# Stick-breaking input projection: the first four weight pieces move into the MLP stage before it

## The reference

```python
for i in range(DEPTH):                      # DEPTH = 2
    h = rmsnorm(x, norm_mix[i])
    ...                                     # mixer: i == 0 latent attention, i == 1 stick-breaking
    x = x + out
    h = rmsnorm(x, norm_mlp[i])
    x = x + jnp.square(jax.nn.relu(h @ mlp_w_up[i])) @ mlp_w_down[i]
y = rmsnorm(x, norm_final)

def sb_mixer(h, q_pos, past_k, past_v, w_in, w_o):
    qkv = (h @ w_in).reshape(B, S, 3, SB_HEADS, SB_HEAD_DIM)
    ...
```

## Time and profile before

| what | value |
|---|---|
| median of three runs (lowest to highest) | 2772.87 us (2772.1 to 2774.59) |
| the profiled execution's own time | 2770.23 us |
| its span, first to last instruction | 2768.4 us |
| TensorE busy | 2665.2 us, 96% of the span, 14531 matmuls |
| VectorE, ScalarE, GpSimd busy | 1733.3, 1155.4 and 732.1 us |
| mean granted TensorE clock | 0.988 of full speed |
| DMA engines busy | 41.5% of the span |

### The profile page before, as it was taken

The page is one execution under the profiler, slowest core; times in us unless marked ns, Lnnn a source line. Parts: engine busy times, 40 slices in busy tenths (PEclk is TensorE's granted clock), DMA queues, the critical chain, the costliest instruction groups (busy, mean ns, idle before and its releaser), DMA issues. The chain is left out here.

```text
span 2768.4 us, 40402 instructions
## 1 busy us (share of the span) xinstructions
PE 2665.2 (96%) x14531; PEld 2236.2 (81%) x14531; DVE 1733.3 (63%) x2331; ACT 1155.4 (42%) x2260; POOL 732.1 (26%) x627
## 2 busy tenths in 40 slices
PE   7989998999999989999899999998999999899998
PEld 6879887788888878888798877776878888788886
DVE  5656666376555688898310008887475555688887
ACT  4334445343333433344322219997343333333433
POOL 3200001135444400001221116665154445300001
PEclk9999999999999999999999999999999999999999
DMA  4311122514444573442235448764234444655342
GB/s 149 88 60 45 45 83 84 190 54 152 137 145 141 189 241 122 160 136 101 86 128 160 145 112 194 174 161 140 91 99 138 145 140 138 235 175 164 126 155 100
DMA packets 285877, 368.81 MB, mean 133 GB/s; under 512 B 25984, under 2 KB 205696, under 8 KB 285696
## 3 DMA queue, kind: packets, MB, share of 16 engines
q1 hardware_dynamic: 285696, 366.42, 41.5%
HBM read 242.19 MB, written 124.16 MB: 132 GB/s over the span
## 5 line engine op out<-in xcount | busy, mean ns | idle before, releaser
L2338 DVE TENSOR_TENSOR x<-m_ps,x 128x1024 f32<-128x1024 f32 x224 | 273.3, 1220 | 92.6 <-PE m_ps L79 92.5
L2047 POOL TENSOR_TENSOR m_u<-m_u,m_u 128x512 f32<-128x512 f32 x128 | 179.5, 1413 | 347.7 <-DVE m_u L2181 342.7
L1994 POOL TENSOR_SCALAR m_stat<-m_stat 128x1 f32<-128x1 f32 x36 | 12.0, 334 | 838.8 <-ACT m_sqjunk L1938 674.4
L2169 DVE TENSOR_TENSOR m_z<-m_ps,m_part 128x512 f32<-128x512 f32 x96 | 66.3, 691 | 143.5 <-PE m_ps L79 143.2
L1800 ACT COPY m_part<-m_ps 128x512 f32<-128x512 f32 x96 | 56.3, 587 | 204.8 <-PE m_ps L79 204.8
L2157 DVE TENSOR_TENSOR m_up<-m_upr,m_up 128x512 fp32r<-128x512 f32 x128 | 87.8, 707 | 28.5 <-ACT m_up L1787 28.5
L3296 ACT ACTIVATE e_b<-e_ps 128x512 f32<-128x512 f32 (+3 forms) x192 | 95.8, 499 | 12.3 <-PE e_ps L3514 11.7
L1787 ACT CAST m_up<-m_upr 128x512 fp32r<-128x512 f32 x128 | 75.6, 615 | 57.9 <-PE m_ps L79 57.9
L3298 ACT ACTIVATE e_ps<-e_ps 128x512 f32<-128x512 f32 (+3 forms) x192 | 96.3, 502 | 0.0
L2027 POOL TENSOR_TENSOR m_uprS<-m_upr 128x512 f32<-128x512 f32 x62 | 94.8, 1529 | 4.9 <-DVE m_upS3l L2157 4.9
L3579 PE MATMUL e_ps<-ident,e_b 128*128 128x128 f32 x576 | 94.7, 274 | 0.7 <-POOL e_b L3394 0.6
(11 more groups left out here) (1192 smaller groups left out, 9183.1 us busy)
## 6 DMA issues: line engine op xcount, KB each, us to landing
scratch_u<-m_u SPq DMA_DIRECT2D x224, 256.0 KB, 2.1
m_ur<-scratch_u SPq DMA_DIRECT2D x208, 256.0 KB, 2.7
m_upr<-in_mlp_w_up SPq DMA_DIRECT2D x32, 1024.0 KB, 5.8
m_wr<-in_mlp_w_down SPq DMA_DIRECT2D x64, 512.0 KB, 6.5
scratch_x<-x SPq DMA_DIRECT2D x18, 512.0 KB, 2.6
x<-scratch_x SPq DMA_DIRECT2D x8, 1024.0 KB, 9.0
scratch_qr<-a_qrst SPq DMA_DIRECT2D x9, 512.0 KB, 3.4
a_x<-in_x_prompt SPq DMA_DIRECT2D x8, 512.0 KB, 4.9
```

What stands on the lines that cost most here:

```text
L2047: pool.tensor_tensor(u_st[out][:], u_st[a][:], u_st[b][:], op).then_inc(u_summed.sem, 1)
L2338: dve.tensor_tensor(out, bank[:, at:at + 2, :], out, ALU.add).then_inc(summed.sem, 1)
```

## The change

Four things are done. SyncE loads pieces 2 and 3 of group 0 in the MLP stage too, behind a wait for product P6 of the last pass (their places in memory are those of operands that P6 is the last to read). ScalarE makes the high parts of pieces 0 and 1 between its last tiles of the MLP stage. GpSimd makes the low part of piece 0 at the end of its MLP program, behind a wait for VectorE's last `scale_2`. In the projection stage the counters of these parts are set by hand, ScalarE makes high parts 2 and 3, and VectorE the low parts of pieces 1, 2 and 3.

```diff
@@ output_and_mlp_stage
-        ahead = [place(f"ahead{j}", shape, raw0_at + 4 * KIB * j) for j in range(2)]
+        ahead = [place(f"ahead{j}", shape, raw0_at + 4 * KIB * j)[:] for j in range(2)]
+        if not final:
+            ahead += [raw[:] for raw, _, _ in next_w[2:]]
...
+        next_in = [] if final else [signal(f"next_in{j}") for j in range(2)]
+        next_hi_done = [] if final else signal("next_hi")
...
                 for j, piece in enumerate(ahead):
-                    sp.dma_start(piece[:], rows[:, 2 * j:2 * j + 2, 0:HALF_TOK]).then_inc(next_in.sem, 16)
+                    if j == 2:
+                        sp.wait_ge(down.sem, down_at(LAST_G, "P6"))
+                    sp.dma_start(piece, rows[:, 2 * j:2 * j + 2, 0:HALF_TOK]).then_inc(next_in[j // 2].sem, 16)
             sp.wait_ge(wt_lo["T1"].sem, CHUNKS)
             sp.dma_start(gain_2[:], next_gain.broadcast_to([P, D_MODEL])).then_inc(gain_2_in.sem, 16)
             if not final:
-                sp.wait_ge(next_in.sem, 32)
+                sp.wait_ge(next_in[1].sem, 32)
                 return
@@ scalar
                 for i in range(5, NT):
                     next_hi(i)
+                    if i < 7:
+                        act.wait_ge(next_in[0].sem, 32)
+                        act.wait_ge(down.sem, down_at(LAST_G, "P4"))
+                        act.copy(next_w[i - 5][1][:], ahead[i - 5]).then_inc(next_hi_done.sem, 1)
@@ gpsimd
+            if not final:
+                pool.wait_ge(next_hi_done.sem, 1)
+                pool.wait_ge(normed_2.sem, NT - len(POOL_SCALES))
+                pool.tensor_tensor(next_w[0][2][:], ahead[0], f32(next_w[0][1][:]), ALU.subtract)
@@ sb_input_stage
         def lo_maker(piece):
-            if piece < PIECES and piece % 2 == 0:
-                return 0, piece // 2 + 1
-            return 1, (piece + 1) // 2 if piece < PIECES else piece - 1
+            return (0, piece + 1) if piece < PIECES else (1, piece - PIECES + 1)
...
-            for piece in range(len(ahead), 2 * PIECES):
+            for piece in range(PIECES, 2 * PIECES):
                 load(piece)
...
-            for piece in range(PIECES):
+            act.sem_inc(w_hi.sem, 2)
+            for piece in range(2, PIECES):
                 weights_hi(piece)
...
-            for piece in range(0, PIECES, 2):
+            dve.sem_inc(w_lo[0].sem, 1)
+            for piece in range(1, PIECES):
                 weights_rest(dve, piece)
```

More of the change, by code:

```diff
@@ L1293, in tokens_split, with output_and_mlp_stage @@
     return raw, (hi, ctx.enter_context(nc.sbuf_tensor(f"{name}_l", [P, KT, TOK], F32R)))
-def output_and_mlp_stage(nc, io, scratch, layer, w_o, first, made, load_x, tokens, next_gain, prompt_out, sample_out):
+def output_and_mlp_stage(nc, io, scratch, layer, w_o, first, made, load_x, tokens, next_w, next_gain, prompt_out,
+                         sample_out):
     final = layer == 1
@@ L1428, in output_and_mlp_stage @@
         hi_2, lo_2 = signal("hi2"), signal("lo2")
-        gain_2_in, next_in, y_out = signal("gain2"), signal("next_in"), [signal(f"yout{u}") for u in range(len(yn))]
+        next_in = [] if final else [signal(f"next_in{j}") for j in range(2)]
+        next_hi_done = [] if final else signal("next_hi")
+        gain_2_in, y_out = signal("gain2"), [signal(f"yout{u}") for u in range(len(yn))]
         def after(engine, sig, count):
@@ L2630, in _ @@
                     next_turn(i)
-    return [piece[:] for piece in ahead]
+    return ahead
 def sb_operands(nc, ctx, name):
@@ L2662, in load_values, with sb_first_weights, sb_input_stage @@
         :, :, bass.ds(p * 2 * SB_DIM, 2 * SB_DIM)]).then_inc(done, 16)
-def sb_input_stage(nc, io, scratch, h_t, sample, ahead, last_rows):
+SB_PIECE = [P, 2, 512]
+def sb_first_weights(nc, at):
+    return [[nc.alloc_sbuf_tensor_at(f"d_w{u}{n}", SB_PIECE, dt, offset=at + (8 * u + skip) * KIB) for n, dt, skip in (
+        ("raw", F32, 4), ("h", F32R, 0), ("l", F32R, 4))] for u in range(4)]
+def sb_input_stage(nc, io, scratch, h_t, sample, ahead, first_w, last_rows):
     WIDTH = 512
@@ L2719, in sb_input_stage @@
             first_pair = sb_operands(nc, late, "d_first")
[L2720 to L2723, removed]
+        w = list(first_w)
+        sb("d_first_w", [P, PIECES * 2 * 2 * WIDTH])
+        sb("d_gap", [P, PIECES * 2 * 2 * WIDTH // 8])
+        for u in range(PIECES, 2 * PIECES):
             hi = sb(f"d_w{u}h", [P, 2, WIDTH], F32R)
@@ L2741, in raw_piece @@
         def raw_piece(piece):
-            return ahead[piece] if piece < len(ahead) else w[piece % (2 * PIECES)][0][:]
+            return ahead[piece] if piece < PIECES else w[piece % (2 * PIECES)][0][:]
         def loads(piece):
             u = piece % (2 * PIECES)
-            return piece // (2 * PIECES) + (u >= len(ahead))
+            return piece // (2 * PIECES) + (u >= PIECES)
         def task_bank(n):
@@ L2822, in weights_hi @@
             def weights_hi(piece):
-                if piece >= len(ahead):
+                if piece >= PIECES:
                     w_in[piece % (2 * PIECES)].wait(act, 16 * loads(piece))
@@ L3670, in build @@
             tokens = tokens_split(nc, first, "h0")
-            ahead = output_and_mlp_stage(nc, io, scratch, 0, io["mla_w_o"][0], first_mla, w_o_made, True, tokens,
+            next_w = sb_first_weights(nc, nc.sbuf_base + 8 * KIB)
+            ahead = output_and_mlp_stage(nc, io, scratch, 0, io["mla_w_o"][0], first_mla, w_o_made, True, tokens, next_w,
                                          io["norm_mix"][1:2, :], [], mla_smp_out)
@@ L3674, in build @@
                 sample = sample_rows(nc, heads, "d")
-                first_pair = sb_input_stage(nc, io, scratch, tokens[1], sample, ahead, sb_rows_out)
+                first_pair = sb_input_stage(nc, io, scratch, tokens[1], sample, ahead, next_w, sb_rows_out)
         first_sb = first_tokens(nc, 1, io["x_at"], io["x_at"] + 140 * KIB)
@@ L3678, in build @@
                                       sb_out, sb_smp_out)
-        output_and_mlp_stage(nc, io, scratch, 1, io["sb_w_o"][0], first_sb, w_o_made, False, None,
+        output_and_mlp_stage(nc, io, scratch, 1, io["sb_w_o"][0], first_sb, w_o_made, False, None, [],
                              io["norm_final"].rearrange("(o d) -> o d", o=1),
```

## The result

The changed kernel takes 2779.93 us (median of 7 runs, 2779.24 to 2784.8), the kernel before, run beside it, 2772.1 (2770.09 to 2774.59): ratio 1.0031, interval 1.0022 to 1.0041. It is slower by 0.3%, some 8 us.

The account below looks back on a forecast made before the run. TensorE, busy 96% of the span, was taken as the bound, so only its idle or slow time at a seam counts. +9.5 + 2.0 - 3.6 = +7.9 us gave a median of 2781 us (+0.28%), range 2776 to 2785.

Parts of the forecast that it names:

- The gain row: Ahead of turn 0: the gain load, queued behind the wait for P6, lands late and leaves TensorE idle, +9.5 us.
- The clock behind the stop: Turn 0 and P5: TensorE runs at the lower 1.2 GHz clock after its idle time, +2.0 us.
- my lower bound of 1.9: Smallest cost in us allowed for the lower clock over turn 0 and P5.
- the upper bound: Largest lower-clock cost over turn 0 and P5: half of a 6 us low stretch, 3.0 us.
- The seam: MLP to projection: TensorE starts 2.28 us earlier, no gap before the fourth piece, first task 6.39 us; -3.6 us.
- the row's 4.3 us at the lower level: First 12 matmuls of the projection's first task, 4.29 us at clock 0.50, assumed to stay so after the change.
- The edits at no cost: MLP tail: ScalarE's casts and GpSimd's low part fit idle time, 0 us; casts would cost 0.3 us uncovered.
- No stop: Rival: gain row in place before turn 0, only the gain at the projection's start remains, 2769.3 us; chance 4%.
- what I called no change: A difference within about 0.2% (5.5 us), which a measurement of this kernel cannot tell from none.
- A short stop: Rival: gain row lands in 3.7 us, projection's first task at the higher clock, +4.0 to +5.5 us; chance 14%.
- A longer stop: Rival: flight of 6.9 us, slow GpSimd product, thin cover uncovered by 1 to 2 us, +10.5 to +14; chance 14%.

Follow-up runs that it names:

- the busy stop: The changed kernel plus 80 TensorE transposes of the identity between P6 and turn 0 of the last pass: 2775.8 us, ratio 1.0014 to the kernel before.
- the gain row first: The changed kernel with the gain row loaded before the wait for P6 and the two piece loads: 2768.88 us, ratio 0.9991 to the kernel before.
- GpSimd's low parts: The kernel with the gain row first, but GpSimd again makes the low parts of pieces 1 and 3 in the projection: 2771.48 us, ratio 0.9994.
- late parts: The kernel with the gain row first, but all parts of pieces 0 and 1 made behind the barrier by ScalarE and VectorE: 2770.63 us, ratio 0.9994.
- late pieces: The kernel with the gain row first, but raw pieces 2 and 3 loaded behind the barrier again: 2771.76 us, ratio 1.0.
- the tail without idle time: The kernel with the gain row first plus extra TensorE transposes of the identity behind turns 4 to 8: 2764.62 us, ratio 0.9978.
- the late gain row: The kernel before with only the gain row's load made to wait for P6 of the last pass: 2780.6 us, ratio 1.0029.

## Why the prediction was right, term by term

The forecast was +7.9 us and slower; the seam shows +7.96, the timed runs +7.8. The mechanism came as forecast. That the sum agrees to 0.1 is luck: the terms are off by -0.57, -0.11 and +0.70, which cancel.

- **The gain row, +9.5 by forecast, +8.97 measured.** The mechanism is shown by the two kernels that move only that load, in and out of the change. The size was off by 0.57 us: from P6's end (1313.57, where SyncE issues and VectorE's add starts together) the gain was issued 0.92 us later and not 1.02, flew for 5.4 us and not 5.8, and GpSimd's product took 2.34 and not 2.41.
- **The clock behind the stop, +2.0 by forecast, +1.89 measured.** Shown by the busy stop, which wins 1.8 back with the stop left in place. Other traces show 1.38 and 2.86 for the same stretch, so the agreement to 0.1 is luck; 1.38 lies under my lower bound of 1.9. The 6 us behind the upper bound were the length of the window that I had chosen; the clock was low there for 6.8 us, from 1333.7 to 1340.5.
- **The seam, -3.6 by forecast, -2.90 in this trace.** TensorE did start about 1.75 us after VectorE's end (1354.81 against 1353.06), and the gap before the fourth piece did go. But I carried the row's 4.3 us at the lower level over to the earlier start, and it was 5.6 us: the first task took 6.83 and not 6.39. And the tail lost 0.25, since the last turn ran at the lower level to its end (1.97 us, 1.60 before). How far the term was mis-sized is not settled. The kernels with the gain row behind the wait but ahead of the pieces, and with the busy stop, have the same edits at the seam; from turn 4 to the second task they take 21.75 and 21.95 us, 22.93 in the changed kernel and with the gain row first, and 25.83 before. By them the term is -4.1 and -3.9. The first of the two has, from its last turn on:

```profile
1351.50 1.77 PE L2634 MATMUL m_ps<-ident,m_yn 128*128 128x128 f32 x8 [0.42 <-DVE m_yn L2429]
1356.37 0.69 PE L77 MATMUL d_ps<-h_h,d_w0h 128*128 128x384 f32 x1 [3.10 <-DVEq L2899]
...
1362.21 0.33 PE L77 MATMUL d_ps<-h_h,d_w0h 128*128 128x384 f32 x1
```

- **The edits at no cost** held: turn 1 to turn 4 takes 10.86 us in both kernels, VectorE has no gap behind ScalarE's casts, and GpSimd's low part ends at 1352.19, ahead of VectorE's 1353.06. That VectorE makes the low parts is worth 0.33 us.
- **The rivals.** No stop: it would have come with the list in another order, and measured 2.8 us faster, inside what I called no change. A short stop: with the gain row ahead of the pieces it comes near, at +5.8 by its median, just over that rival's +5.5. A longer stop: no run shows one, and the flight was 5.4 us and not 6.9. The clock's upper bound of 3.0, which I had kept for the end of the range, was almost reached in one trace (2.86).

By the Trainium skill's page on transfers ("DMA: Bandwidth & Descriptors", Anatomy of one DMA) the third piece of 512 KB would land 5.6 us after the first issue, an estimate; here it was 0.92 + 5.4 = 6.3, nearer to the rows than to the rule. The page fits that rule on transfers that GpSimd issues, which the prediction does not say; these are SyncE's. Its other statement, that a wait is served by the sequencer that issues, is what the trace shows: the three loads left one behind the other when P6 ended.

Open: what decides when the clock rises. In the changed kernel, with the gain row first, with GpSimd's low parts and with the late parts it fell in the tail and stayed low for 17.1 us, until the middle of the first task. In the two kernels with 5.84 us, with the late pieces and before, it rose in the last turn (in the busy stop at its end), and fell again between 2.6 us ahead of the first task (before) and 0.3 us into it (the busy stop). The rows ahead are nearly the same, and the traces do not show why.

## What to carry to other kernels

A wait put in front of one transfer held every later transfer of SyncE's list: before adding one, list what stands behind it and when each is wanted, and move ahead what doesn't need the wait. A stop of TensorE cost more than its length, here 1.4 to 2.9 us more for 6 to 9 us of idle time. At a seam where TensorE must wait anyway the clock is a term of its own beside the operands that are made ready early: 0.7 to 1.9 us here, against 2.9 to 4.1. Cheap work that kept TensorE busy ahead of the seam brought it in. And where a term rests on the clock, one trace does not size it: the same code gave 6.83 and 5.84 us for one task.

## What the runs showed of the hardware that was not expected

- An idle time of 2.33 us, just after the clock had risen, was followed by its fall, 0.6 us after TensorE had gone on (late pieces); one of 1.73 us behind a busy tail was not (the tail without idle time).
- The lower level lasted between 3.4 and 6.1 us after TensorE's start behind idle times of 3.1 to 5.5 us, without following their length: behind 5.4 us it was 3.4 (late parts) and 6.1 (the kernel before with the late gain row), behind 3.1 us it was 3.4 (late pieces) and 5.6 (the changed kernel).
- From its fall in the tail to its rise in the first task the clock was low for 17.1 us in each of four traces, though TensorE started the task 2.3 us later in one of them (late parts).
- A transfer of 512 KB landed in 3.4 us alone (the late gain row in the kernel before: issued at 1319.03), in 4.2 with two behind it, in 5.4 with two ahead.
